# Expert layers of a two-layer diffusion step: 64 prompt tokens by fetched rows in both layers, in place of 128 in the second

## The reference

```
def peer_ffn(h, w_query, sub_keys, u_tab, v_tab):
    q = (h @ w_query).reshape(B, L, PEER_HEADS, 2, PEER_QDIM // 2)
    s = jnp.einsum('blhtd,htnd->blhtn', q, sub_keys).astype(F32)
    s1, i1 = lax.top_k(s[..., 0, :], PEER_TOPK)
    s2, i2 = lax.top_k(s[..., 1, :], PEER_TOPK)
    ...
    top, pos = lax.top_k(cand, PEER_TOPK)
    idx = jnp.take_along_axis(cidx, pos, axis=-1)
    g = jax.nn.softmax(top, axis=-1).astype(h.dtype)
    ...
        act = jax.nn.gelu(jnp.einsum('td,tkd->tk', hx, u_tab[ix]))
        return jnp.einsum('tk,tkd->td', gx * act, v_tab[ix])
```

## Time and profile before

| | |
|---|---|
| median of 3 runs | 3007.42 us |
| the profiled execution | 3013.17 us, span 3011.4 us |
| TensorE matmul busy | 2676.7 us, 89% of the span |
| VectorE busy | 2256.0 us, 75% |
| ScalarE busy | 1221.3 us, 41% |
| GpSimd busy | 490.6 us, 16% |
| DMA | 649.62 MB, mean 216 GB/s |
| expert slots of layer 0 | 679 to 1553 us |
| expert slots of layer 1 | 2248 to 2979 us |

### The profile page before, as it was taken

How to read it: one execution, slowest core, us unless ns; L and a number is a source line. 1 busy time by engine, 2 the same in 40 slices (tenths; PEclk the granted TensorE clock), 3 DMA queues, 4 the chain that set the end, 5 groups by cost and what they waited for, 6 DMA issues and landing times. The chain is left out here.

```text
span 3011.4 us, 44269 instructions
## 1 busy us (share of the span) xinstructions
PE 2676.7 (89%) x16509; PEld 2380.7 (79%) x16509; DVE 2256.0 (75%) x4330; ACT 1221.3 (41%) x1811; POOL 490.6 (16%) x356
## 2 busy tenths in 40 slices
PE   7976898999999999999989897896778999999765
PEld 4964798999999999998868777796667888888544
DVE  8876688984335999887873565489977888888887
ACT  3344443873333333333334223443654444444322
POOL 0000151000000000000000000152323333344552
PEclk9997899999999999999988898898999999999997
DMA  5721343666446777776751323144889999999995
GB/s 214 280 76 44 117 132 98 241 253 214 155 153 208 255 252 247 240 248 200 228 194 34 122 98 119 54 137 147 299 310 342 344 347 346 346 357 345 309 332 192
DMA packets 331815, 649.62 MB, mean 216 GB/s; under 512 B 187216, under 2 KB 190032, under 8 KB 324320
## 3 DMA queue, kind: packets, MB, share of 16 engines
q1 hardware_dynamic: 289280, 470.79, 46.3%
q0 software_dynamic: 36864, 134.23, 12.1%
q10 hardware_dynamic: 5472, 41.95, 3.5%
HBM read 577.97 MB, written 68.91 MB: 215 GB/s over the span
## 5 line engine op out<-in xcount | busy, mean ns | idle before, releaser
L1988 PE MATMUL pe_s<-hl_hi,pq_uh 128*128 128x384 f32 (+1 forms) x2304 | 738.7, 321 | 42.1 <-DVE pq_ul L163 22.3
L1989 PE MATMUL pe_s<-hl_lo,pq_uh 128*128 128x384 f32 (+1 forms) x2304 | 727.3, 316 | 0.0
L1990 PE MATMUL pe_s<-hl_hi,pq_ul 128*128 128x384 f32 (+1 forms) x2304 | 726.8, 315 | 0.0
L1988 PEld LDWEIGHTS pe_s<-hl_hi,pq_uh 128*128 128x128 f32 x2304 | 445.5, 193 | 64.9 <-issue 32.5
L2061 PE MATMUL peer_acc<-val_vh,val_wh 128*128 128x512 f32 x1280 | 408.2, 400 | 86.7 <-DVE val_wl L163 86.4
L163 DVE TENSOR_TENSOR val_vl<-val_vr,val_vh 128x1024 fp32r<-128x1024 f32 x256 | 312.7, 1221 | 223.3 <-ACT val_vh L2179 222.3
L1989 PEld LDWEIGHTS pe_s<-hl_lo,pq_uh 128*128 128x128 f32 x2304 | 446.1, 194 | 8.2
L1990 PEld LDWEIGHTS pe_s<-hl_hi,pq_ul 128*128 128x128 f32 x2304 | 445.3, 193 | 0.0
L2221 POOL TENSOR_TENSOR pq_ul<-pq_ur,pq_uh 128x512 fp32r<-128x512 f32 x96 | 125.6, 1331 | 1921.9 <-ACT pq_uh L2079 1921.8
L2061 PE MATMUL peer_acc<-val_vh,val_wl 128*128 128x512 f32 x1280 | 402.2, 396 | 0.0
L2061 PE MATMUL peer_acc<-val_vl,val_wh 128*128 128x512 f32 x1280 | 401.9, 396 | 0.0
(11 more groups left out here) (476 smaller groups left out, 3984.3 us busy)
## 6 DMA issues: line engine op xcount, KB each, us to landing
pq_ur<-in_peer_u SPq DMA_DIRECT2D x256, 512.0 KB, 3.7
val_vr<-in_peer_v SPq DMA_DIRECT2D x256, 512.0 KB, 5.0
gates<-gate_stg ACTq DMA_DIRECT2D x34, 1024.0 KB, 8.1
val_mrow<-in_ada_rows SPq DMA_DIRECT2D x56, 512.0 KB, 4.7
val_gr<-gates SPq DMA_DIRECT2D x128, 192.0 KB, 4.7
pq_ur<-in_w_query SPq DMA_DIRECT2D x32, 512.0 KB, 3.5
s_wv<-val_out SPq DMA_DIRECT2D x32, 512.0 KB, 5.5
val_gr<-gates SPq DMA_DIRECT2D x128, 128.0 KB, 7.3
```

Of the source, the lines that this page charges most:

```text
L1988: pe.matmul(o, r32(uh[:, b, k]), r32(hi[:, k, a:T]), start=k == 0, stop=False)
L1989: pe.matmul(o, r32(uh[:, b, k]), r32(lo[:, k, a:T]), start=False, stop=False)
L1990: mm = pe.matmul(o, r32(ul[:, b, k]), r32(hi[:, k, a:T]), start=False, stop=k == KC - 1)
```

## The change

Both layers get the same plan: 64 prompt tokens take the fetched way, the other 64 prompt tokens and the 256 latent tokens are dense (320 columns). A fetched token lies on two partitions, n and n + 64; each of the two takes one half of its 128 experts, so that one indirect DMA still brings 128 rows, and 64 DMAs for u and 64 for v are enough in a layer. The indices and gates of the second half are moved to the upper partitions by two small DMAs on GpSimd's queue, h is put on both halves by matmuls, and `add_experts` adds the two halves with a folding matrix. The fetch ring has 3 rows instead of 5. The gate stage has 14 groups for 40 chunks in both layers, with 16 fetched rows in it; the other 112 are spread over the 128 slots (0.875 per slot). The ring has 36 blocks: 92 slots have a product and a value step, 36 a value step alone.

In the value step the first 64 dense tokens fill only half a tile. Their low and their high half lie side by side in one 128-wide stationary operand, which meets the high and the low half of v: 4 matmuls for them instead of 6. With two full tiles that makes 16 matmuls of 512 columns per slot, where it was 18 in layer 0 and 12 in layer 1.

```
 class Plan:
 
 
-    ROWS = P
-    def __init__(self, fetched):
-        self.fetched = fetched
-        self.first = TP if fetched else 0
-        self.tokens = T - self.first
-        self.tiles = range(self.first // P, NT)
+    def __init__(self, fetched, groups):
+        self.fetched = self.first = fetched
+        self.folded = fetched == HALF
+        self.tokens = T - fetched
+        self.tiles = range(fetched // P, NT)
         self.chunks, self.parts = self.tokens // CT, self.tokens // HALF
-        groups = [2] * 16 if fetched else [3 if g % 6 == 2 else 2 for g in range(22)]
         self.spans = [range(sum(groups[:g]), sum(groups[:g + 1])) for g in range(len(groups))]
         assert self.spans[-1].stop == self.chunks
         self.last = GATED + len(groups)
         self.ring = self.last + TAIL
         self.fetches = [[] for _ in range(self.last + NB)]
-        if fetched:
-            n = 2 * self.ROWS
-            early = 2 * len(groups)
-            for i in range(n):
-                at = GATED + i // 2 if i < early else self.last + (i - early) * NB // (n - early)
-                self.fetches[at].append(i)
+        n = 2 * fetched
+        early = n // 8
+        for i in range(n):
+            at = GATED + i * len(groups) // early if i < early else self.last + (i - early) * NB // (n - early)
+            self.fetches[at].append(i)
+    def half(self, part):
+        return (part + self.parts) % 2
+PLANS = Plan(64, [3] * 12 + [2] * 2), Plan(64, [3] * 12 + [2] * 2)
...
-    plan = Plan(layer == 1)
+    plan = PLANS[layer]
...
+RING_ROWS = 3, 3
 class Fetch:
 
 
-    RING = 5
     def __init__(self, s, plan, layer):
-        self.layer, self.n = layer, 2 * plan.ROWS
+        self.RING = RING_ROWS[layer]
+        self.layer, self.n = layer, 2 * plan.fetched
...
-        wh, wl = x.sb("wh", [P, 2, TOKENS]), x.sb("wl", [P, 2, TOKENS])
+        pair = x.sb("w", [P, 2, 2 * TOKENS])
+    edge = HALF if plan.folded else 0
+    wh, wl = pair[:, :, edge:edge + TOKENS], pair[:, :, TOKENS:2 * TOKENS]
...
-                        mm = pe.transpose(acc[:, 4 + k // 4, k % 4 * P:(k % 4 + 1) * P], nm.h[:, k, 0:P], cx.ident)
+                        out = acc[:, 4 + k // 4, k % 4 * P:(k % 4 + 1) * P]
+                        if plan.folded:
+                            pe.matmul(out[0:HALF], nm.h[:, k, 0:HALF], cx.ident, start=True, stop=True)
+                            mm = pe.matmul(out[HALF:P], nm.h[:, k, 0:HALF], cx.ident, start=True, stop=True)
+                        else:
+                            mm = pe.transpose(out, nm.h[:, k, 0:P], cx.ident)
...
-                for t in plan.tiles:
+                if plan.folded:
+                    for rhs in (vh, vl):
+                        for c in range(2):
+                            pe.matmul(acc[:, c, :], r32(pair[:, b, 0:P]), r32(rhs[:, b, c * 512:(c + 1) * 512]),
+                                      start=False, stop=False, skip_group_check=True)
+                for t in range((FROM + HALF) // P, NT):
...
+                if plan.folded:
+                    pool.dma_start(ft.index[HALF:P, 0:HALF], ft.index[0:HALF, HALF:P]).then_inc(ft.moved, 16)
+                    pool.wait_ge(ft.moved, 16)
-                    b, k = i % ft.RING, i % plan.ROWS
+                    if i == ft.RING and plan.folded:
+                        pool.wait_ge(ft.gated, 1)
+                        pool.dma_start(ft.gate[HALF:P, 0:HALF], ft.gate[0:HALF, HALF:P]).then_inc(ft.shared, 16)
+                    b, k = i % ft.RING, i % plan.fetched
...
-                lo_part(nc, wl[:, b], A[:, z.place(ahead)], wh[:, b]).then_inc(wlow, 1)
+                if plan.folded:
+                    lo_part(nc, pair[:, b, 0:HALF], A[:, z.place(ahead), 0:HALF], wh[:, b, 0:HALF])
+                lo_part(nc, wl[:, b, edge:TOKENS], A[:, z.place(ahead), edge:TOKENS], wh[:, b, edge:TOKENS]).then_inc(wlow, 1)
...
-        out = s.sb("out", [P, NT, D])
+        out, fold = s.sb("out", [P, NT, D]), s.sb("fold", [P, HALF])
...
+                        if n < 2 and plan.folded:
+                            pe.matmul(tr[:, n % 2, j * P:j * P + HALF], total[:, cols], fold[:], start=True, stop=True)
+                            mm = pe.matmul(tr[:, n % 2, j * P + HALF:(j + 1) * P], out[:, 0, cols], fold[:], start=True, stop=True)
```

More of the change, by code:

```diff
@@ L1827, in __init__ @@
         self.gate, self.act, self.weight = (s.sb(x, [P, P]) for x in ("fgate", "fact", "fw"))
-        self.turned, self.copied, self.indexed = (s.sem(f"f_{x}") for x in ("h_turned", "h_copied", "indexed"))
+        self.turned, self.copied, self.indexed, self.gated, self.moved, self.shared = (
+            s.sem(f"f_{x}") for x in ("h_turned", "h_copied", "indexed", "gates", "index_moved", "gates_moved"))
         self.loaded = [s.sem(f"f_row{b}_loaded") for b in range(self.RING)]
@@ L1934, in _ @@
                 if n == RING:
-                    sp.wait_ge(gst1, 16 * (PARTS // 2))
+                    sp.wait_ge(gst1, 16 * ((PARTS + 1) // 2))
                     gate(0, 0)
@@ L2104, in gates @@
                 part, at = c * CT // HALF, c * CT % HALF
-                half = part % 2
+                half = plan.half(part)
                 if at == 0 and part >= 2:
@@ L2122, in store_piece @@
                     act.wait_ge(evacd, c + 1)
-                half, keys = part % 2, slice(k * SOON, (k + 1) * SOON)
+                half, keys = plan.half(part), slice(k * SOON, (k + 1) * SOON)
                 if half == 0 and k < PIECES:
@@ L2162, in expert_gelu @@
                 for half in range(2):
-                    end = plan.ROWS // 2 * (half + 1)
+                    end = plan.fetched // 2 * (half + 1)
                     if end - 1 in plan.fetches[slot]:
-                        cols = slice(end - plan.ROWS // 2, end)
+                        cols = slice(end - plan.fetched // 2, end)
                         act.wait_ge(ft.used, end)
@@ L2223, in _ @@
                 pool.wait_ge(ft.indexed, 1)
+                if plan.folded:
+                    pool.dma_start(ft.index[HALF:P, 0:HALF], ft.index[0:HALF, HALF:P]).then_inc(ft.moved, 16)
+                    pool.wait_ge(ft.moved, 16)
                 for i in range(ft.n):
-                    b, k = i % ft.RING, i % plan.ROWS
+                    if i == ft.RING and plan.folded:
+                        pool.wait_ge(ft.gated, 1)
+                        pool.dma_start(ft.gate[HALF:P, 0:HALF], ft.gate[0:HALF, HALF:P]).then_inc(ft.shared, 16)
+                    b, k = i % ft.RING, i % plan.fetched
                     if i >= ft.RING:
                         pool.wait_ge(ft.used, i - ft.RING + 1)
-                    table = d["peer_rows"] if i < plan.ROWS else d["peer_v"]
+                    table = d["peer_rows"] if i < plan.fetched else d["peer_v"]
                     nc.gpsimd.indirect_dma_start(ft.rows[:, b], None, table.rearrange("l a b m -> (l a b) m"),
@@ L2354, in _ @@
             if plan.fetched:
-                st.done(v.tensor_scalar(ft.weight[:], pick[:, 1, 0:P], float(NKEYS), float(layer * NKEYS * NKEYS), ALU.mult, ALU.add))
+                own_rows = slice(0, plan.fetched)
+                st.done(v.tensor_scalar(ft.weight[own_rows], pick[own_rows, 1, 0:P], float(NKEYS), float(layer * NKEYS * NKEYS), ALU.mult, ALU.add))
                 st.settle()
-                v.tensor_tensor(ft.index[:], ft.weight[:], pick[:, 0, 0:P], ALU.add).then_inc(ft.indexed, 1)
+                v.tensor_tensor(ft.index[own_rows], ft.weight[own_rows], pick[own_rows, 0, 0:P], ALU.add).then_inc(ft.indexed, 1)
             fill()
@@ L2372, in _ @@
                 dve.wait_ge(picked, 1)
-                st.done(v.tensor_scalar(ft.gate[:], pick[:, 2, 0:P], 1.0 / GATE_SCALE, None, ALU.mult))
+                v.tensor_scalar(ft.gate[own_rows], pick[own_rows, 2, 0:P], 1.0 / GATE_SCALE, None, ALU.mult).then_inc(ft.gated, 1)
                 dve.wait_ge(ft.copied, 1)
@@ L2383, in fetched @@
             def fetched(i):
-                b, k = i % ft.RING, i % plan.ROWS
+                b, k = i % ft.RING, i % plan.fetched
                 row = ft.rows[:, b]
                 dve.wait_ge(ft.loaded[b], 16 * (i // ft.RING + 1))
-                if i < plan.ROWS:
+                if i < plan.fetched:
                     v.scalar_tensor_tensor(row, row, 1.0, ft.h[:], ALU.mult, ALU.mult, accum_out=ft.act[:, k:k + 1]).then_inc(ft.used, 1)
                     return
-                if k % (plan.ROWS // 2) == 0:
-                    half = k // (plan.ROWS // 2)
-                    cols = slice(k, k + plan.ROWS // 2)
+                if k % (plan.fetched // 2) == 0:
+                    half = k // (plan.fetched // 2)
+                    cols = slice(k, k + plan.fetched // 2)
                     dve.wait_ge(ft.curved, half + 1)
+                    dve.wait_ge(ft.gated, 1)
+                    if plan.folded:
+                        dve.wait_ge(ft.shared, 16)
```

(3 more changed lines are left out.)

13 lines of the change are left out of this document (8 added, 5 removed).

## The result

The changed kernel takes 3079.32 us (median of 4 runs, 3073.89 to 3086.82), the kernel before 3010.19 us beside it (median of 4, 3006.27 to 3015.5). The ratio is 1.0232, with a 95% interval of 1.0212 to 1.0253: slower, by 69 us. The forecast was 3080 us. Of 17 more executions of the kernel before, beside which the experiments stand, two took 3724.7 and 4374.35 us at a lower granted clock (0.674 and 0.553); such slow ones are left out of every ratio. The profiled execution took 3079.34 us, 66.2 more than the one of before.

What follows compares the result with a forecast made beforehand. It took TensorE to bound layer 0's slots and transfers layer 1's. Layer 0's -4.8 and layer 1's +77.3 gave +72.5 on the profiled 3013.2, 3085.7 us; less 5.8 for the median, 3080 us, range 3047 to 3110.

Steps and rivals of the forecast that it cites:

- Layer 1's slots: Layer 1: TensorE sets 92 slots at 7.16 us and 36 tail slots take 4.0 each, 802.7 against 730.4: +72.3 us.
- The reason given for 4.0: Layer 1's tail: a block of v's way in comes last; between 3.64 and 4.69 us, nearer layer 0's tail of 4.13.
- Layer 0's slots: Layer 0: VectorE's list, 8.52 us in slots 34 to 63, eats TensorE's saving; 873.9 against 874.6: -0.7 us.
- rival A: Both layers: TensorE sets every slot, so layer 0 changes by -84.9 us and layer 1 by +59.3; 2983 us, chance 0.04.
- The tail's step: Layer 0's last 36 slots: VectorE's list takes 4.46 us in 31, about 4.3 in five, against TensorE's 3.64; 159.8 us.
- Gate stage of layer 0: Layer 0 before its slots: fewer chunks and tables on VectorE -10.3 us, products before slot 0 -1.
- Small terms: Outside the slots: h on both halves +4.2 and +2.1 us, end +3 per layer, products before slot 0 -1 and +1.
- B: TensorE in both layers: a matmul of 320 columns costs what one of 256 does, 0.120 us; 2994 us, chance 0.03.
- C: Tails of both layers: the ring of 3 rows is too short, so they stay at 4.69 us; 3114 us, chance 0.12.

## Why the prediction was right

**Layer 1's slots (+72.3, measured +72.3).** Right in mechanism: transfers relieved, TensorE next, and its slot a full microsecond longer than the old one. Two terms were off and cancelled, which is luck: the two values agree better than their parts. The 92 slots with a product took 667.2 us, not 658.7; a steady slot is 7.18, and the first ones waited some 7 us for gates and v. The 36 of the tail took 135.9 us, 3.77 each, not 4.0: close to TensorE's own 3.64, with TensorE 97% busy. The reason given for 4.0 does not hold. It leaned on layer 0's tail of 4.13 us as if a block's way in had set it, but that tail was TensorE's, 18 matmuls of 0.2272 us = 4.09, and at a DMA share of 0.73 (kernel before):

```profile
1375.00:1550.00 175.00, 174.39 (x766) 142.88 (x765) 143.56 (x217) 62.11 (x84) 0.00 (x0) 1.00 0.73 217
```

In the changed kernel's tail of layer 1 (2908 to 3044 us) `val_vh` waited for TensorE a little more than for the transfer:

```profile
ACT val_vh L2199 <- PE peer_acc L2081: 38.6, 19, 2.2
ACT val_vh L2199 <- DMA val_vr<-in_peer_v: 32.1, 15, 3.5
```

**Layer 0's slots (-0.7, measured -1.2).** Right in mechanism for slots 34 to 83, shown from three sides: taking work from TensorE gives nothing there, making VectorE's rows cheap gives 23 us, moving them away 33. That TensorE would gain all of its 84 us (rival A) was wrong, and the reason given for its 0.04, a list that would fit if it were spread, is borne out in part: with the rows moved, slots 64 to 83 fall to 7.19 us, slots 34 to 63, with their three builds, to 7.58. Here too two parts cancelled, by luck. The 92 slots with a product took 707.5 us where 714.1 was worked out, since the list was priced too high in slots 34 to 83 (404.2 us for 413.4). The 36 of the tail took 166.1, 4.61 each, where 159.8 was. Of the 84 us that TensorE alone would have saved, 46 went in slots 34 to 83 and 35 in the tail.

The tail's step is the one that was wrong in its cause: VectorE's list alone was named. VectorE was 93% busy there, at a DMA share of 0.93 and with TensorE at 83%, so it was near its limit, but shortening its list by cheap rows gave 2.5 us of 166, and VectorE's waits for gates rose from 10.5 to 30.7 us, and placing 16 builds ahead of it gave 1 to 3. The tail of layer 1 in the same kernel has the same plan and as many bytes of v, gates and rows per slot, but no builds, and takes 3.77 us per slot; the 0.84 us between them is what comes with the builds (and with the last `modulate` operations, in four slots). Whether they cost it by VectorE's time or by their own transfers (eight stores of 512 KB between 1400 and 1500 us) was not isolated.

**Gate stage of layer 0 (-11.3, measured -6.3).** A mis-sized term. VectorE's part, from its first one-hot table to the end of the last group's list, fell from 143.0 to 134.8 us, 8.2 instead of 10.3. Part of the gap is VectorE waiting for TensorE's use of its tables, now that nearly all groups have three chunks:

```profile
580.05 0.69 DVE L2450 TENSOR_TENSOR gates_eq<-g_iota,gates_i 128x1024 f16<-128x1024 f16 x1 [1.34 <-PE peer_acc L2024]
```

There are three such waits, 3.9 us; before there were three of 1.0 us in all. The way from there to the first value step grew by 2 us, where the prediction had 1 us less.

**Small terms.** Putting h on both halves was counted at +4.2 us in layer 0 and was hidden by the ranking (-0.6). The end was counted at +3 and took +0.4. The first and the gate stage nearly cancel: -7.1 predicted for layer 0's stages ahead of its slots, -8.5 measured, 1.6 of that in a part that nothing touched. Between the two profiled executions 72.5 us were worked out and 66.2 came, by the medians it was 69; that 3080 us meets 3079.32 so closely is luck.

**Rivals B and C.** Three matmuls of 320 columns in 0.44 us exclude B. VectorE had next to no idle time before the sums over fetched rows (62 operations each for the two accumulators), and none of its waits is for a row, so the ring of 3 rows was long enough, and C is excluded. The Trainium skill (TensorE: Matmul & The Clock Gate, Back-to-back issue gap) gives 131 ns for a matmul of 512 columns in a sustained stream. The changed kernel does not agree: with TensorE full at a clock of 1.00, 16 of them took 2503.10 - 2499.44 = 3.66 us, 229 ns each.
